# Block one's attention: values with ones as the stationary operand, sums of the probabilities from TensorE

## The reference, cut to what matters

```python
def blocked_gqa(q, k, v):                 # q: 8 heads of 64; k, v: 2 heads of 64; 512 tokens, Q_BLOCK = 128
    def one_block(qi):
        s = jnp.einsum("bqgrd,bkgd->bgrqk", qi, k)
        p = jax.nn.softmax(s, axis=-1)
        return jnp.einsum("bgrqk,bkgd->bqgrd", p, v)
...
attn_out = blocked_gqa(q, k, v)
mixed = jnp.concatenate([attn_out, ssd_out], axis=-1)
x = x + jnp.einsum("ble,ed->bld", mixed, w_out[i])
```

## Time and profile before

| | us |
|---|---|
| median of three runs | 3146.48 |
| the runs | 3138.63, 3146.48, 3146.72 |
| the profiled execution | 3142.69 |
| its span in the trace | 3140.9 |
| layer one's `FirstMix`, roughly | 16 to 284 |
| layer two's, roughly | 695 to 958 |

### The profile page before, as it was taken

The page is one execution under the profiler, slowest core; times in us unless marked ns, Lnnn a source line. Parts: engine busy times, 40 slices in busy tenths (PEclk is TensorE's granted clock), DMA queues, the critical chain, the costliest instruction groups (busy, mean ns, idle before and its releaser), DMA issues. The chain is left out here.

```text
span 3140.9 us, 37997 instructions
## 1 busy us (share of the span) xinstructions
PE 3025.9 (96%) x15290; PEld 2632.7 (84%) x15290; DVE 1923.5 (61%) x2891; ACT 1125.7 (36%) x1669; POOL 89.3 (3%) x72
## 2 busy tenths in 40 slices
PE   7989999999999999999998899999999999999998
PEld 5778888887788888899986499999999978788886
DVE  5755775856664878766646755543554365488674
ACT  4454422234453222343346123221222345343232
POOL 0031000000040000000000000000000000000000
PEclk9998999999998999999999899999999999999999
DMA  3110554521102655512110121121121210245432
GB/s 127 54 34 27 186 172 142 196 89 61 48 14 91 198 180 187 165 64 101 63 33 18 41 95 61 61 69 57 63 66 63 95 50 1 79 169 200 169 132 83
DMA packets 79546, 298.78 MB, mean 95 GB/s; under 512 B 8555, under 2 KB 12203, under 8 KB 78220
## 3 DMA queue, kind: packets, MB, share of 16 engines
q1 hardware_dynamic: 79372, 296.35, 28.0%
HBM read 287.93 MB, written 8.39 MB: 94 GB/s over the span
## 5 line engine op out<-in xcount | busy, mean ns | idle before, releaser
L122 PE MATMUL banks<-normed_hi,weights_hi 128*128 128x512 f32 (+2 forms) x2320 | 843.1, 363 | 0.8 <-DVE normed_lo L561 0.8
L123 PE MATMUL banks<-normed_lo,weights_hi 128*128 128x512 f32 (+2 forms) x2320 | 840.2, 362 | 0.0
L104 ACT ACTIVATE weights_hi<-weights_raw 128x1024 fp32r<-128x1024 f32 (+3 forms) x365 | 395.4, 1083 | 1221.4 <-PE banks L125 1178.3
L125 PE MATMUL banks<-normed_hi,weights_lo 128*128 128x512 f32 (+2 forms) x2320 | 737.8, 362 | 0.0
L110 DVE TENSOR_TENSOR weights_lo<-weights_raw,weights_hi 128x1024 fp32r<-128x1024 f32 (+3 forms) x365 | 463.0, 1269 | 145.4 <-ACT weights_hi L104 140.7
L123 PEld LDWEIGHTS banks<-normed_lo,weights_hi 128*128 128x128 f32 x2320 | 438.4, 189 | 41.2
L122 PEld LDWEIGHTS banks<-normed_hi,weights_hi 128*128 128x128 f32 x2320 | 437.0, 188 | 42.7 <-DVE normed_lo L561 1.2
L125 PEld LDWEIGHTS banks<-normed_hi,weights_lo 128*128 128x128 f32 x2320 | 429.6, 189 | 41.0
L122 PE MATMUL banks<-hidden_hi,weights_hi 128*128 128x512 f32 (+1 forms) x880 | 323.1, 367 | 0.1
L123 PE MATMUL banks<-hidden_lo,weights_hi 128*128 128x512 f32 (+1 forms) x880 | 323.0, 367 | 0.0
L125 PE MATMUL banks<-hidden_hi,weights_lo 128*128 128x512 f32 (+1 forms) x880 | 294.7, 367 | 0.0
(11 more groups left out here) (447 smaller groups left out, 4246.9 us busy)
## 6 DMA issues: line engine op xcount, KB each, us to landing
weights_raw<-in_w_up SPq DMA_DIRECT2D x176, 512.0 KB, 3.3
ada_tiles<-in_ada SPq DMA_DIRECT2D x96, 512.0 KB, 3.3
weights_raw<-in_w_down SPq DMA_DIRECT2D x64, 704.0 KB, 4.0
weights_raw<-in_w_in SPq DMA_DIRECT2D x67, 512.0 KB, 3.3
up_rows<-in_up_rows SPq DMA_DIRECT2D x44, 512.0 KB, 3.4
weights_raw<-in_w_out SPq DMA_DIRECT2D x32, 512.0 KB, 3.2
x_kept<-x SPq DMA_DIRECT2D x2, 3072.0 KB, 11.0
x<-x_kept SPq DMA_DIRECT2D x1, 3072.0 KB, 10.1
```

The lines of the kernel that those rows point to most:

```text
L104: act.activation(self.hi[:, n % 2, 0:w], self.raw[:, n % 2, 0:w], ACT.Copy).then_inc(self.high_ready, 1)
L122: pe.matmul(out, self.hi[:, s, m], xh, start=k == 0, stop=False)
L123: pe.matmul(out, self.hi[:, s, m], xl, start=False, stop=False)
L125: mm = pe.matmul(out, self.lo[:, s, m], xh, start=False, stop=k == kt - 1)
```

## The change

`mix` swaps its operands. The stationary operand is now the values, widened by ones: `vt` has 192 columns for each block of 128 keys, the first head's 64 values, 64 ones, the second head's 64 values, and step n takes columns 0 to 127 (even n) or 64 to 191 (odd n). The moving operand is the turned probabilities, 128x128. The product therefore comes out with features on 64 partitions and the queries along the row, and on the other 64 partitions stands the sum of the probabilities of each query, repeated. `back` and its bank go, as does `accum_out` of the exponential. `rows` runs once for a pair instead of once for a step: two reciprocals and two products, each of 64x128, the inverse written to the other half of the partitions than it was read from. Pairs take turns in the two banks 5 and 6. `high` and `low` come one odd step earlier. A memset writes the ones once in a layer.

```diff
@@ FirstMix.COUNTS, __init__
+        self.vt = buf("v_tokens", [P, LT, 3 * 64])
+        self.ot = buf("out_rows", [P, 2, P])
+        self.inv = buf("inverse_sums", [P, 2, P])
@@ rope_scalar: the values' copy leaves the middle columns
+        act.activation(self.vt[:].rearrange("p t (n c) -> p t n c", n=3)[:, :, 0:3:2],
+                       self.bank(BANK_OUT).rearrange("p (t n c) -> p t n c", t=LT, n=2),
                        ACT.Copy).then_inc(on["v_copied"], 1)
@@ rope_vector
+        step.step(dve.memset(self.vt[:, :, 64:P], 1.0))
@@
+    def out(self, p):
+        return self.bank(BANK_OUT + p % 2)[:, 0:2 * P].rearrange("p (m c) -> p m c", m=2)
@@ attention_tensor
         def mix(n):
             self.wait(pe, "turned_copied", n + 1)
-            if n:
-                self.wait(pe, "token_rows", n)
-            else:
+            p, m = n // 2, n % 2
+            if n == 0:
                 self.wait(pe, "v_copied", 1)
-            r, o = 64 * (n % 2), self.bank(BANK_OUT)[:, 0:64]
+            if m == 0 and p >= 2:
+                self.wait(pe, "token_rows", p - 1)
+            o = self.out(p)[:, m]
             for t in range(LT):
-                mm = pe.matmul(o, self.pt[:, n % 2, t], self.vt[:, t, r:r + 64], start=t == 0, stop=t == LT - 1)
+                mm = pe.matmul(o, self.vt[:, t, 64 * m:64 * m + P], self.pt[:, m, t], start=t == 0, stop=t == LT - 1)
             mm.then_inc(on["mixed"], 1)
-        def back(p):
-            self.wait(pe, "token_rows", 2 * p + 2)
-            if p:
-                self.wait(pe, "out_lo", p)
-            pe.transpose(self.bank(BANK_BACK)[:, 0:P], self.ot[:, p % 4],
-                         K["ident"]).then_inc(on["out_turned"], 1)
@@ attention_scalar
-                           scale=self.scale(n), accum_out=self.sm[:, n % 4, 2:3]).then_inc(on["exp"], 1)
+                           scale=self.scale(n)).then_inc(on["exp"], 1)
@@ attention_vector
-        def rows(n):
-            s, p = self.sm[:, n % 4], n // 2
-            self.wait(dve, "mixed", n + 1)
-            dve.reciprocal(s[:, 3:4], s[:, 2:3]).then_inc(on["sum_inverted"], 1)
-            self.wait(dve, "sum_inverted", n + 1)
-            if p >= 4:
-                self.wait(dve, "out_turned", p - 3)
-            dve.tensor_scalar(self.ot[:, p % 4, 64 * (n % 2):64 * (n % 2) + 64],
-                              self.bank(BANK_OUT)[:, 0:64], s[:, 3:4], None,
-                              ALU.mult).then_inc(on["token_rows"], 1)
+        def rows(p):
+            o, inv, out = self.out(p), self.inv[:, p % 2], self.ot[:, p % 2]
+            first, second = self.HEADS
+            self.wait(dve, "mixed", 2 * p + 2)
+            dve.reciprocal(inv[first], o[second, 0])
+            dve.reciprocal(inv[second], o[first, 1]).then_inc(on["sum_inverted"], 1)
+            self.wait(dve, "sum_inverted", p + 1)
+            if p >= 2:
+                self.wait(dve, "out_hi", p - 1)
+            dve.tensor_tensor(out[first], o[first, 0], inv[first], ALU.mult)
+            dve.tensor_tensor(out[second], o[second, 1], inv[second], ALU.mult).then_inc(on["token_rows"], 1)
```

More of the change, by code:

```diff
@@ L1518 @@
     COUNTS = {"k_squared": 5, "head_sums": 5, "k_root": 1, "k_inverted": 1, "k_spread": 1, "k_normed": 1, "q_root": 1,
-              "q_inverted": 1, "swapped": 5, "roped": 5, "rope_step": 15, "pair_hi": 5, "pair_lo": 5, "v_turned": 1, "v_copied": 1,
+              "q_inverted": 1, "swapped": 5, "roped": 5, "rope_step": 16, "pair_hi": 5, "pair_lo": 5, "v_turned": 1, "v_copied": 1,
               "scores": STEPS, "max": STEPS, "max_step": STEPS, "exp": STEPS, "turned": STEPS, "turned_copied": STEPS,
-              "mixed": STEPS, "sum_inverted": STEPS, "token_rows": STEPS, "out_turned": 16, "out_hi": 16, "out_lo": 16,
+              "mixed": STEPS, "sum_inverted": 16, "token_rows": 16, "out_hi": 16, "out_lo": 16,
               "pads": 1, "first_tap": 8, "tap": 24, "conv_done": 8, "conv_silu": 2, "z_silu": 1, "dt_abs": 1, "dt_turned": 1,
@@ L1789, in swap @@
             if i == 0:
-                self.wait(pe, "rope_step", 4)
+                self.wait(pe, "rope_step", 5)
             pe.matmul(self.bank(BANK_SCORES + i % 2), self.swaps[:, min(i, 1)], self.qkv[:, i], start=True,
@@ L1959, in attention_tensor @@
                 mix(n - 1)
-            if n % 2 and n >= 5:
-                back((n - 5) // 2)
         yield self.slot(STEPS)
         mix(STEPS - 1)
-        for p in range((STEPS - 1 - 5) // 2 + 1, STEPS // 2):
-            yield self.slot(STEPS) + 0.5 + 0.3 * (p - STEPS // 2 + 2)
-            back(p)
     def attention_scalar(self, act):
@@ L1986, in high @@
             m, qt = p // 4, p % 4
-            self.wait(act, "out_turned", p + 1)
-            act.activation(self.att_hi[:, m, qt * P:(qt + 1) * P],
-                           self.bank(BANK_BACK)[:, 0:P],
+            self.wait(act, "token_rows", p + 1)
+            act.activation(self.att_hi[:, m, qt * P:(qt + 1) * P], self.ot[:, p % 2],
                            ACT.Copy).then_inc(on["out_hi"], 1)
@@ L2003, in attention_scalar @@
                 copy(n)
-            if n % 2 and n >= 5:
+            if n % 2 and n >= 3:
                 yield self.follows(n, 0.6, 0.42)
-                high((n - 5) // 2)
-        for p in range((STEPS - 1 - 5) // 2 + 1, STEPS // 2):
-            yield self.slot(STEPS) + 0.65 + 0.3 * (p - STEPS // 2 + 2)
-            high(p)
+                high((n - 3) // 2)
+        yield self.slot(STEPS) + 0.65
+        high(STEPS // 2 - 1)
     def attention_vector(self, dve):
@@ L2018, in top @@
                 self.wait(dve, "q_inverted", 1)
-            if n >= 4:
-                self.wait(dve, "token_rows", n - 3)
             dve.tensor_reduce(s[:, 0:1], self.bank(BANK_SCORES + n % 2), AX.X, ALU.max).then_inc(on["max_step"], 1)
@@ L2048, in attention_vector @@
                 top(n + 2)
-            if n:
+            if n and n % 2 == 0:
                 yield self.follows(n, 0.35, 0.35)
-                rows(n - 1)
-            if n % 2 and n >= 5:
+                rows(n // 2 - 1)
+            if n % 2 and n >= 3:
                 yield self.follows(n, 0.7, 0.55)
-                low((n - 5) // 2)
+                low((n - 3) // 2)
         yield self.slot(STEPS) + 0.3
-        rows(STEPS - 1)
-        for p in range((STEPS - 1 - 5) // 2 + 1, STEPS // 2):
-            yield self.slot(STEPS) + 0.75 + 0.3 * (p - STEPS // 2 + 2)
-            low(p)
+        rows(STEPS // 2 - 1)
+        yield self.slot(STEPS) + 0.75
+        low(STEPS // 2 - 1)
     def aux_room(self, pe, u):
```

8 lines of the change are left out of this document (2 added, 6 removed).

## The result

The changed kernel takes 3156.3 us in the median of 5 runs (3155.2 to 3163.4); the kernel before takes 3143.9 us in the runs beside it (3138.6 to 3146.7). The ratio is 1.0045, with a 95% interval from 1.0029 to 1.0060: slower, by 9 to 19 us. The forecast of 3156 us was met. Whether its steps were is another question, and the answer is mixed.

A forecast was written before the change was run, and what follows sets the result against it. PE, with work in flight 96% of the span, was taken as the bound; layer one's +4.8, layer two's +3.0 and the clock's +2 summed to +9.8 us, giving 3156 us after profile-to-median adjustment, range 3141 to 3168 us.

The forecast's parts named there:

- place 1: Convolution's end: the reciprocal block delays the taps, ACT's Silu and the B tile; +2.8 us layer one, +1.0 layer two.
- PE's +0.4 a layer: Between projection tiles: wider mix less the dropped back, about half hidden in PE's waits; +0.4 us a layer (0 to 0.8).
- the clock's +2: Layer one's longer pause for the B tile lowers PE's clock once; +2 us (0 to 3.4 for each layer).
- place 2: Gates' Silu: the block ahead of the first diagonal delays ACT's unbroken chain to PE's longest wait; +1.9 us a layer.
- place 3: Beside the SSD heads: the block ahead of the skip delays the weighing PE needs; +1.0 us a layer.
- place 4: Tail: PE starts the output projection sooner, then waits at its fourth tile; -1.3 us a layer (-3 to 0).
- block's length: A pair's two reciprocals (0.91 us each) and two products on DVE, less 0.05 us overlap: 2.35 us.
- cover of 0.87 us: Convolution's end, layer one: a table load holds the Silu until 163.51, absorbing 0.87 us of the taps' 3.7 us delay.
- rival 3: Backlog adds up, DVE bounds the convolution's end, clock falls in both layers and one tail; +20 us, 3166 us; chance 0.20.
- short block: A block of 1.1 us, if a 64x128 reciprocal takes 0.3 us like a product; tail -2.5 us a layer.
- PE's own term: Each mix of eight products streams 128 columns instead of 64; 0.06 us more per mix, 64 of them: +3.8 us.
- rival 1: Not slower, the reciprocal is cheap at 0.3 us for 64x128; -4 us, 3142 us; chance 0.15.

The follow-up runs named there:

- three places moved: Changed kernel, DVE's block moved behind the convolution's taps and first diagonal, last high and low ahead of last scaling: 3142.6 us; with one-head pieces as well, 3126.4 us.
- cheap kernel: The changed kernel with each of a pair's two long reciprocals replaced by a multiplication of the same 64x128 by a constant: 3131.3 us, ratio 0.9955.

## Why the prediction was right, and where only by luck

The forecast was +9.8 us by its sum; the spans give +17.4 (16.7 at the last marker on DVE), the medians +12.4. Term by term, with what the stretches of the table show for both layers together:

| term | forecast | measured |
|---|---|---|
| place 1, with PE's +0.4 a layer and the clock's +2 | +6.6 | +13.5 (7.9 and 5.7) |
| place 2, gates' Silu | +3.8 | +4.5 (2.3 and 2.3) |
| place 3, beside the heads | +2.0 | +4.0 (2.6 and 1.4) |
| place 4, the tail | -2.6 | -3.3 (-1.6 and -1.7) |
| ahead of the attention, between the layers and behind them | 0 | -2.1 |

**The block's length** was right: 0.955 for 0.91 and 2.58 for 2.35. The Trainium skill (VectorE: DVE Perf Modes, First, the fixed hardware budget) gives a repeat count of 8, by which I had estimated 8.3 ns a column; from 204 ns at 8 columns to 955 at 128 the trace has 6.3. The rule of its section Two Vector instructions with no wait between them agrees with the trace: the operands of the four start at different partitions, and none starts before the one ahead has ended (152.12 + 0.96 is 153.08, the next starts at 153.09).

**Place 2** was right in its mechanism and nearly in size, +2.3 us for each layer against +1.9. The difference is the longer block, 2.58 - 0.38 = 2.2. Moving the block behind the first diagonal took this away: +2.3 becomes -0.4 in both layers.

**Place 1 is the term that failed**: 13.5 us where the sum had 6.6. I began with the block at 150.40 us as if nothing ahead of it were late, and it starts at 152.12. I had put what the earlier pairs leave behind at nothing. Against the marker at 79, DVE's taps come 0.9 us late at 88 to 91 us and its maximum at 94 us is in time again, but from 103 us on the maxima stay 1.4 us or more late, and the one at 143 us is 2.6 late. PE waits 2.09 us at 113.59 where it waited 0.58, and the wait for x_dt grows from 0.54 to 1.49. DVE then reaches the last taps 6.3 us late, where I had 3.7, since to the 1.7 us of backlog come two blocks of 2.2 each. ACT's Silu, 163.51 in the earlier trace rows, starts now at

```profile
166.11 1.28 ACT L1695 ACT_TABLE_LOAD   x1
168.98 1.92 ACT L1695 ACTIVATE conv<-conv 128x2048 f32<-128x2048 f32 x1 [1.59 <-DVE conv L1738]
```

5.5 us later. The cover of 0.87 us by the table load was right. In layer two the step of the earlier trace rows did absorb the first block, as forecast: the maximum there is 12.7 us late and so was the one at 815 us, ahead of the block. But 12.7 is already 2.8 more than at 757 us. So the same backlog, 2.6 and 2.8 us, is missing in both layers, and layer two pays +5.7 where I had +1.0, PE's +0.4 and half of the clock. This was rival 3, the backlog that adds up, at this place though not in the whole.

**The clock** fell where I had expected it, behind the wait for the B tiles, but also ahead of it. Behind it, from the B tile to the B and C products, PE takes 1.6 us more than before, in layer two as well: 3.2 us where the sum had 2. The fall ahead of it also costs PE time, 3.8 us between `turn` at 147.31 and the B tile, less the 1.4 that the wait has grown. But these 2.4 us lie in front of a wait that ends on ACT, and ACT runs from its Silu at 168.98 to the B tile without a pause, so they only shorten that wait and are no cost of their own. The windows around both waits, which stand at 1.00 in the kernel before:

```profile
145.00:155.00 10.00, 7.73 (x30) 6.73 (x30) 8.28 (x15) 4.37 (x7) 2.04 (x2) 0.66 0.14 52
175.00:182.00 7.00, 6.75 (x31) 5.97 (x32) 4.28 (x8) 1.97 (x4) 0.00 (x0) 0.76 0.21 75
```

With three places moved, the first window still stands at 0.66, but the B tile waits 1.9 us instead of 3.6 and the seven microseconds behind it run at full clock.

**Place 3** had the right sign and half the size, 4.0 us for 2.0 (2.6 in layer one, 1.4 in layer two). I costed the block ahead of the skip, but the later weighing also stands otherwise to GpSimd's products. Before, 14 of the 16 weighings overlap such a product too, but are always first to start, and none takes over 1.22 us (mean 1213 ns). Now (mean 1315 ns) some start while the product is under way, and once in a layer the weighing takes 2.02 us. DVE first, then GpSimd, in the trace of after:

```profile
251.29 2.02 DVE L2307 TENSOR_TENSOR diagonal<-diagonal,bc_scores 128x1024 f32<-128x1024 f32 x1
```
```profile
250.73 1.51 POOL L2390 TENSOR_TENSOR scaled_c<-conv,decay_rows 128x384 f32<-128x384 f32 x1 [1.44 <-ACT decay_rows L2222]
252.19 1.98 POOL L2391 TENSOR_TENSOR scaled_c<-conv,decay_rows 128x384 f32<-128x384 f32 x1
```

PE's longest wait beside the heads, 1.75 us at 253.37, ends on this weighing. The kernel with the block moved beside the heads has six such weighings of 2.0 us, each begun some 0.5 us behind a product of GpSimd. Still, that the two hold each other up is read from their overlap and was not tried apart.

**Place 4** came near the number with other parts. PE did start the projection sooner and waited at its fourth tile, as forecast, for 3.7 us. Against the last heads the tile comes 3.0 us sooner (forecast 2.1), and 2.1 us of that are the norm at a less low clock (11.0 us before, 8.9 now), which was not in the sum. Behind the wait the clock is low again and 1.4 us are lost. The cheap kernel shows what the block does here: -7.6 us in that stretch without it, -1.6 with it, as the norm takes 6.9 us there and the wait 1.6. So the block costs 6 us in the tail, where I had reckoned 1.2 (-2.5 for the short block, -1.3 for the long).

**PE's own term**, 0.06 us for a `mix`, was wrong in the other direction. Ahead of a projection tile eight products of 128 columns take 0.81 us (the median of 32 places), as in the earlier trace rows with 64: the low end of my range. At other places, ahead of the norm for one, they take 0.89, where the kernel before has 0.84 ahead of its `back`s.

So the number stands because two errors cancel. By the ratios, the change without its reciprocals gains 14 us (rival 1 had 4), and the reciprocals cost 28 (rivals 1 and the forecast were 14 apart). I had reckoned the parts of both too small by about the same amount, 10 and 14 us.

## What to carry to other kernels

An engine that is 61% busy still has no room for a long piece of work in the wrong spot: the same 43 us of DVE work (the reciprocals less the multiplications of the cheap kernel) cost 28 us as one block of 2.6 us in every second step, and nothing that can be seen as pieces of 1.25 us in each step with three places moved. When work is added to an engine that others wait for, follow its backlog from the first addition on, not from the last place before the wait; and look for the first link of every chain that the engine feeds before moving the piece in front of it. An edit that removes or narrows PE work ahead of a slow stretch should be costed with the clock of that stretch at both levels, since wider products there can come out ahead.

## What the runs showed that I had not expected

- Twice the moving columns in every `mix` made the kernel 14 us faster (0.9954). The granted clock of the twenty microseconds around layer one's norm went from 0.61 and 0.50 to 0.82 and 0.67. Ahead of a projection tile the width itself costs nothing: 0.81 us for eight either way.
- A reciprocal on DVE costs 0.955 us for 128 columns on 64 partitions out of PSUM, 0.945 on 128 partitions out of SBUF, some 3.3 times a product of 64x128 (0.289).
- A power on GpSimd takes 20.8 us for 128x128.
